# Latent attention: where GpSimd turns the next head's queries in its queue

## The reference

```python
def mla(u, w_in, q_norm, w_qb, kv_norm, w_kvb, w_out):
    ...
    q = (rms_norm(cq, q_norm) @ w_qb).reshape(B_, S, B_HEADS, B_NOPE + B_ROPE)
    q_nope, q_rope = q[..., :B_NOPE], q[..., B_NOPE:]
    kv = (rms_norm(ckv, kv_norm) @ w_kvb).reshape(B_, S, B_HEADS, B_NOPE + B_VDIM)
    k_nope, v = kv[..., :B_NOPE], kv[..., B_NOPE:]
    ...
    q_rope = rotate(q_rope, cos[:, None, :], sin[:, None, :])
    ...
        logits = (jnp.einsum('bqhd,bshd->bhqs', qn_b, k_nope)
                  + jnp.einsum('bqhr,bsr->bhqs', qr_b, k_rope)).astype(jnp.float32) * scale
        probs = jax.nn.softmax(logits, axis=-1)
        return jnp.einsum('bhqs,bshd->bqhd', probs.astype(v.dtype), v)
    ...
    return (o * jax.nn.silu(z)) @ w_out
```

## Time and profile before

| | us |
|---|---|
| median of 3 runs | 2795.02 (2794.20 to 2795.81) |
| the profiled execution | 2794.93 |
| its span, first to last instruction | 2793.6 |
| PE busy | 2697.8 |
| VectorE busy | 1683.9 |
| ScalarE busy | 1388.7 |
| GpSimd busy | 910.7 |
| GpSimd's scaling L1780, 128 times | 144.3, 1.127 each |

### The profile page before, as it was taken

How to read it: one execution, slowest core, us unless ns; L and a number is a source line. 1 busy time by engine, 2 the same in 40 slices (tenths; PEclk the granted TensorE clock), 3 DMA queues, 4 the chain that set the end, 5 groups by cost and what they waited for, 6 DMA issues and landing times.

```text
span 2793.6 us, 36562 instructions
## 1 busy us (share of the span) xinstructions
PE 2697.8 (97%) x13692; PEld 2250.3 (81%) x13692; DVE 1683.9 (60%) x2861; ACT 1388.7 (50%) x2550; POOL 910.7 (33%) x745
## 2 busy tenths in 40 slices
PE   8999989999999999999998999998999999999997
PEld 7878878777788888888886778777788888888886
DVE  6767775643288888887557875556552444443344
ACT  5768864435367767775346335542442343334222
POOL 0434441223366655563122221123541111111431
PEclk9999999999999999999999999999999999999999
DMA  3101132221100000003211310033342110010242
GB/s 136 42 31 42 42 125 70 85 83 39 38 13 10 11 11 10 11 31 113 74 48 35 114 38 23 23 128 106 113 147 93 47 33 29 31 31 31 83 151 76
DMA packets 62367, 167.68 MB, mean 60 GB/s; under 512 B 7024, under 2 KB 15856, under 8 KB 61040
## 3 DMA queue, kind: packets, MB, share of 16 engines
q1 hardware_dynamic: 62192, 165.34, 17.3%
HBM read 139.10 MB, written 26.21 MB: 59 GB/s over the span
## 4 chain that ended last, share of the span: by engine, by line
PE 88%; DVE 5%; ACT 3%; POOL 2%; issue 1%; DMA 0%; POOLq 0%; ACTq 0%; DVEq 0%
PE ps L344 82%; PE ps L462 4%; PE ps L3012 1%; PE ps L788 1%; ACT t L328 1%; POOL t L1328 1%; POOL t L1332 1%; POOL t L1780 0%; DVE t L3370 0%; DMA t<-in_wflat 0%; DVE t L2338 0%; DVE t L919 0%; DVE t L888 0%; POOL t L1330 0%; DVE t L1907 0%
## 5 line engine op out<-in xcount | busy, mean ns | idle before, releaser
L344 PE MATMUL ps<-t,t 128*128 128x512 f32 (+8 forms) x11804 | 2539.4, 374 | 71.3 <-POOL t L2691 10.3
L344 PEld LDWEIGHTS ps<-t,t 128*128 128x128 f32 (+4 forms) x11804 | 2049.5, 185 | 491.4 <-issue 67.4
L335 POOL TENSOR_TENSOR t<-t,t 128x1024 fp32r<-128x1024 f32 (+2 forms) x151 | 323.8, 2145 | 1102.8 <-ACT t L328 746.8
L328 ACT ACTIVATE t<-t 128x1024 fp32r<-128x1024 f32 (+2 forms) x187 | 167.9, 898 | 413.0 <-PE ps L344 412.5
L1720 DVE TENSOR_TENSOR t<-ps,t 128x512 fp32r<-128x512 f32 x256 | 164.6, 684 | 33.2 <-ACT t L1628 32.0
L1780 POOL TENSOR_SCALAR t<-t,t 128x1024 f32<-128x1024 f32 x128 | 144.3, 1127 | 118.7 <-DVE t L1726 113.7
L462 PE MATMUL ps<-t,t 128*128 128x128 f32 x1176 | 157.5, 274 | 11.9 <-POOL t L1780 9.6
L462 PEld LDWEIGHTS ps<-t,t 128*128 128x128 f32 x1176 | 132.4, 140 | 31.1 <-issue 15.2
L1733 DVE TENSOR_REDUCE t<-ps 128x1 f32<-128x1024 f32 x128 | 154.2, 1205 | 0.6 <-PE ps L344 0.6
L1636 ACT ACTIVATE t<-ps,t 128x1024 f32<-128x1024 f32 x128 | 143.0, 1117 | 3.5 <-DVE t L1733 3.3
L1628 ACT ACTIVATE t<-ps 128x512 fp32r<-128x512 f32 x256 | 139.1, 591 | 9.8 <-PE ps L462 5.8
(11 more groups left out here) (245 smaller groups left out, 2538.8 us busy)
## 6 DMA issues: line engine op xcount, KB each, us to landing
t<-in_wflat SPq DMA_DIRECT2D x138, 512.0 KB, 3.6
t<-in_wada SPq DMA_DIRECT2D x48, 256.0 KB, 4.8
t<-in_wflat SPq DMA_DIRECT2D x9, 1024.0 KB, 5.9
t<-in_xT SPq DMA_DIRECT2D x16, 512.0 KB, 7.3
md<-t SPq DMA_DIRECT2D x30, 256.0 KB, 2.7
t<-md SPq DMA_DIRECT2D x30, 256.0 KB, 3.9
t<-in_wflat SPq DMA_DIRECT2D x32, 128.0 KB, 2.0
hd<-t SPq DMA_DIRECT2D x8, 512.0 KB, 3.1
```

The source lines that it names most:

```text
L328: ac.activation(parts(i)[0][:, 0:n], raw[i % 2][:, 0:n], ACT.Copy).then_inc(*on.up(ac, "whi", i))
L335: e.tensor_tensor(lo[:, 0:n], raw[i % 2][:, 0:n], hi[:, 0:n], ALU.subtract) \
L344: return pe.matmul(o, l, r, start=start, stop=stop)
```

## The change

GpSimd's steps for the next head are called one iteration later. In the loop of `gpsimd` inside `stage_attn_b`:

```diff
                     if i >= 5 and i % 2:
                         gated((i - 5) // 2)
                     if i in pair_step and pair_step[i][1] == 1:
                         w_lo(po, HV[pair_step[i][0]] + 2)
-                    if i in head_step:
-                        head_po(*head_step[i])
+                    if i - 1 in head_step:
+                        head_po(*head_step[i - 1])
```

## The result

The changed kernel takes 2808.97 us (median of 6 runs, 2803.95 to 2813.04); the kernel before took 2795.07 us beside it (6 runs, 2793.61 to 2796.51). The ratio is 1.0047, with a 95% interval of 1.0037 to 1.0056: slower by 0.4 to 0.6%. The profiled execution took 2803.95 us, its span is 2802.6 us.

The account below looks back on a forecast made before the run. PE, busy 97% of the span, was taken to bound the kernel. Even heads 3.5, odd heads 4.8, head 1 -0.8 and head 15 +1.5 made +9.0 on 2794.9: 2803.9 us, range 2798 to 2813.

Parts of the forecast that it names:

- The moved wait: Latent attention: PE's wait for POOL's scaling leaves block 18 (gain 0.3 us) for blocks 19 (odd heads) and 27 (even, 0.3).
- The hold of L1770 and L1332: Odd heads: VectorE's key subtraction holds the turn's last operation on POOL 0.4 us, making 0.8 us a head instead of 0.45.
- The sum: All heads: seven even 3.5 us, six odd 4.8, first head -0.8, last head +1.5, together +9.0 us.
- Step 3: Even heads: the later 384-column split for the next odd head's query weights makes PE wait 0.2 us, seven times.
- First halves: Turns of the queries' first halves end before their next readers; tightest, VectorE's temporary buffer in even heads, by 0.2 us.
- Head 15: Last head: a 1024-column split of 2.41 us before the second half's turn delays scaling; loss of 1.5 us.
- Rival (c): More follows than added up: VectorE's buffer margin fails or L1770 waits, PE waits again; 2811 or 2808 us, chance 26%.
- Head 1: First head: no product in the way, no turn before its first scaling; PE gains 0.8 us.

## Why the prediction was right, point by point

The forecast was 2803.9 us, range 2798 to 2813, slower with 0.80. Measured: 2809.0 and, once more, 2805.4. The waits stand where the forecast had put them (0.85 us at block 19, 0.28 at block 27), and the distance between heads of the same parity grew by 1.38 us where 1.3 were forecast.

- **The moved wait.** Right in place and size. Blocks 19 and 27 were named, with a shift of 0.8 and 0.3 us; measured 0.81 and 0.31. The gain of 0.3 at block 18, with VectorE's L1720 behind it, is 0.36.
- **The hold of L1770 and L1332.** 0.4 us forecast; L1332 took 0.37 longer, and taking the meeting away gave 0.37 back. The sum counted the hold only where the turn meets L1770; in the run with the splits alone L1770 meets a scaling instead, and there it costs 0.3 us through VectorE. The Trainium skill's rule (page "SBUF — State Buffer", section "SBUF: two separate sides") that whichever of the two starts first locks the other out for its whole length is what the trace shows here, in both directions, to within 0.15 us: VectorE was done 0.51 us behind the start of L1332, which took 0.37 us more.
- **Step 3.** Forecast 0.2, measured 0.27 us; seven times, the difference is 0.5 us. The forecast set the first matmul of the next queries, at 956.4, as the moment of need. What waits is the load of its weights, which stands at 956.17 in the kernel before; with the change the same load comes 0.4 us late (955.51, counted from the start of the scores at 953.89), and the matmuls behind it 0.27 us. First before, then after:

```profile
956.17 2.03 PEld L344 LDWEIGHTS ps<-t,t 128*128 128x128 f32 x9
```

```profile
955.51 1.91 PEld L344 LDWEIGHTS ps<-t,t 128*128 128x128 f32 x9 [0.41 <-issue]
```

- **First halves.** Right except in head 15: VectorE's margin at the temporary buffer held, by 0.26 to 0.41 us in heads 2 to 14.
- **Head 15.** Forecast +1.5, measured +4.0 us; this term was mis-sized. Its timeline in the changed kernel:

```profile
1244.53 0.69 DVE L1322 TENSOR_TENSOR t<-ps,t 32x512 f32<-32x512 f32 x1 [0.61 <-POOL t L1332]
...
1252.33 1.29 POOL L1328 TENSOR_TENSOR t<-t,t 32x512 f32<-32x512 f32 x1
1252.53 1.64 DVE L1770 TENSOR_TENSOR t<-t,t 64x512 fp32r<-64x512 f32 x1
...
1253.68 0.95 POOL L1330 CAST t<-t 32x512 fp32r<-32x512 f32 x1
...
1257.33 1.39 PE L462 MATMUL ps<-t,t 128*128 128x128 f32 x8 [2.47 <-POOL t L1780]
...
1258.37 2.91 PE L344 MATMUL ps<-t,t 96*128 96x512 f32 x6
```

I had added up the second half alone, and had called an even head's margin the tightest. The first half of head 15 has a 1024-column split in its queue as well (iteration 113), so the turn ends after VectorE wants the buffer: 0.61 us. With it PE and the sum are late by 0.57 us. L1770 is held by the turn's first operation (1.64 us instead of 0.68) and holds the cast behind it (0.95 instead of 0.60). The run with only step 1 moved has this second part without the first and at full clock, and loses 1.85 us in head 15: the 1.5 of the forecast and 0.35 for the cast. What is left of the 4.0, 1.6 us, is the stretch at half clock behind the wait. Rival (c) of the prediction came true in one head.
- **Head 1.** Forecast -0.8. From PE's first scores to the blocks of head 1 the trace gives -2.4, of which 1.6 is the stretch at half clock that only before had: -0.8.
- **The sum.** Forecast +9.0 us. By the measured terms: 7 x (0.31 + 0.27) = 4.1, 6 x 0.81 = 4.9, head 1 -2.4 and head 15 +4.0, together 10.6, against 10.5 between the anchors. That the profiled run's 2803.95 us hit the forecast is partly luck. The terms of the queue came out 1.5 us larger than forecast, most of it in head 15. Against that the run had two stretches at half clock fewer than the run of before (near 371 and 758 us) and one more (in head 15), 1.8 us less in all.
- **The rest to the medians.** The prediction set the profiled run of before equal to the median, right for before, and left out that the new kernel's runs could have another share of half clock. That is 1.5 us in one measurement and 5.0 in the other, as much as the largest term of the sum.

## What to carry to other kernels

In an engine that works in order, ask of a step that is moved what it will stand behind, not only what it no longer stands in front of: here the turn passed one scaling and landed behind a product that waits for another engine, and a split went with it. The same turns moved as far but ahead of that product, with the splits left where they were, gain 5 us instead of losing 9 to 14. Do the sum for the odd ones out (first and last head, where the pieces have other sizes) with all their pieces, and compare kernels whose runs spread by a few us at the same granted clock.

## What the runs showed of the hardware

- A VectorE operation with two SBUF inputs and a GpSimd operation hold each other in either order: L1770 (0.68 us) took up to 1.64, GpSimd's L1332 (1.29) 1.66, its scaling L1780 (1.12) 1.45. It was enough that one came 0.17 us ahead of the other. In each meeting the later one was longer by what the earlier one had left to run, less 0.11 to 0.15 us; before, L1770 at 911.12 overlapped the scaling that ended at 911.25 and took its usual 0.68. VectorE's L1720, with one input in PSUM, ran beside the scaling in its usual 1.28 us (908.13).
- A wait of PE for a split weight stands in the profile as "issue" of the weight load (0.41 us) and not as a wait for GpSimd; it was found by the shift of the blocks behind it.
- Stretches at half clock, of 3.4 us or some of them in a row, stand in all eleven traces, most at the same work in each (near 350, 1500, 1820, 1940, 1960 and 2550 us in the kernel before). A few come in some traces only, and one of these in the stage cost PE 1.6 us; three or four are worth as much as half of this effect.
